# Interleaving the cross-attention output projection with the sample attention in a four-layer hybrid decoder, with one more weight slot

## The reference, cut to what matters

```python
for layer in range(DEPTH):                       # 4
    xn = rmsnorm(x, norm_mix_g[layer])
    out = rg_block(xn, ...) if layer % 2 == 0 else gla_block(xn, ...)
    x = x + out
    x = x + cross_attn(rmsnorm(x, norm_xa_g[layer]), mem_k[layer], mem_v[layer], xa_wq[layer], xa_wo[layer])
    hid = rmsnorm(x, norm_mlp_g[layer]) @ mlp_w1[layer]
    x = x + jnp.square(jax.nn.relu(hid)) @ mlp_w2[layer]

def cross_attn(xn, k, v, w_q, w_o):              # 4 heads of 256, 256 memory tokens
    q = (xn @ w_q).reshape(B, T, XA_HEADS, XA_HD)
    s = jnp.einsum('bthd,bmhd->bhtm', q, k.astype(q.dtype)).astype(jnp.float32) * (XA_HD ** -0.5)
    p = jax.nn.softmax(s, axis=-1).astype(xn.dtype)
    o = jnp.einsum('bhtm,bmhd->bthd', p, v.astype(xn.dtype)).reshape(B, T, D_MODEL)
    return o @ w_o
```

## Time and profile before

| | |
|---|---|
| time of the runs | 6314.46 and 6902.73 us, median 6608.6 |
| profiled execution | 6308.44 us; its slowest core spans 6306.9 us |
| TensorE (PE) busy | 4477.8 us, 71% |
| VectorE (DVE) busy | 3094.6 us, 49% |
| ScalarE (ACT) busy | 1959.9 us, 31% |
| GpSimd (POOL) busy | 449.1 us, 7% |
| read from and written to HBM | 452.87 MB and 35.68 MB |

### The profile page before, as it was taken

One profiled execution on the slowest core, in us unless ns is written; L12 is line 12 of the kernel. 1 busy time (PEld: TensorE's weight loads), 2 busy tenths in 40 slices (PEclk: granted clock), 3 DMA queues, 4 the chain that ended last, 5 costly groups with the idle time before them and its releaser, 6 DMA issues.

```text
span 6306.9 us, 78782 instructions; the slowest of 8 cores (6271.5 to 6306.9 us)
## 1 busy us (share of the span) xinstructions
PE 4477.8 (71%) x24832; PEld 2232.8 (35%) x24832; DVE 3094.6 (49%) x5724; ACT 1959.9 (31%) x3361; POOL 449.1 (7%) x824
## 2 busy tenths in 40 slices
PE   4443394999855569399984448499985556849996
PEld 2111143444433334344431123344433333334443
DVE  0165662545544446255565556155554444625554
ACT  2365631211322223121136654121132222412113
POOL 0111101000000000100011110100000000010000
PEclk6677695899977779599986679599987777959997
DMA  7501126222222221621210111612122222161221
GB/s 159 108 6 9 13 30 102 43 34 41 26 45 45 45 47 21 106 43 28 41 18 8 11 26 23 115 27 41 28 26 45 45 45 50 28 110 28 41 34 57
DMA packets 286689, 283.22 MB, mean 45 GB/s; under 512 B 70176, under 2 KB 219072, under 8 KB 286288
## 3 DMA queue, kind: packets, MB, share of 16 engines
q0 software_dynamic: 229616, 210.47, 22.8%
q1 hardware_dynamic: 38240, 50.92, 2.5%
q10 hardware_dynamic: 18432, 16.79, 0.9%
HBM read 452.87 MB, written 35.68 MB: 77 GB/s over the span
## 4 chain that ended last, share of the span: by engine, by line
PE 58%; DMA 17%; ACT 9%; DVE 8%; issue 7%; POOL 1%; DVEq 0%; ACTq 0%; SPq 0%; POOLq 0%
PE ps L305 56%; ACT tf L282 5%; DMA wslot<-ck 4%; DVE tf L292 3%; DMA o_Ss<-Sfs 3%; DMA wslot<-cv 2%; DMA wslot<-rg_w_in 2%; ACT L282 2%; PE ps L313 1%; ACT tb L282 1%; DVE Sb_p L292 1%; DMA o_mv<-tf 1%; DVE tf L783 1%; DMA wslot<-rg_w_a 1%; DMA wslot<-xa_wo 1%
## 5 line engine op out<-in xcount | busy, mean ns | idle before, releaser
L305 PE MATMUL ps<-xnT,wslot 128*128 128x512 bf16 (+2 forms) x9040 | 1892.1, 369 | 15.5 <-DVE tf L292 15.5
L305 PE MATMUL ps<-tb,wslot 128*128 128x512 bf16 (+2 forms) x5536 | 1079.5, 350 | 564.0 <-POOL tb L296 329.2
L282 ACT ACTIVATE tb<-ps 128x512 bf16<-128x512 f32 (+3 forms) x1074 | 572.7, 542 | 2536.4 <-PE ps L305 1763.4
L305 PEld LDWEIGHTS ps<-xnT,wslot 128*128 128x128 bf16 (+1 forms) x9040 | 854.9, 103 | 974.7 <-issue 224.7
L285 DVE TENSOR_TENSOR xT<-xT,ps 128x512 f32<-128x512 f32 (+1 forms) x1600 | 941.3, 605 | 446.7 <-PE ps L305 417.6
L305 PEld LDWEIGHTS ps<-tb,wslot 128*128 128x128 bf16 x5536 | 494.0, 98 | 1119.9 <-issue 613.2
L285 DVE TENSOR_TENSOR tb<-tb 128x512 bf16<-128x512 bf16 (+1 forms) x640 | 244.8, 385 | 736.1 <-ACT tb L282 733.2
L305 PE MATMUL ps<-actT,wslot 128*128 128x512 bf16 (+1 forms) x2560 | 486.3, 354 | 4.7 <-DMA wslot<-xa_wo 4.7
L305 PE MATMUL ps<-tb 128*128 128x8 bf16 (+4 forms) x1470 | 194.1, 230 | 263.8 <-DVE tb L288 183.8
L313 PE MATMUL ps<-identb,wslot 128*128 128x128 bf16 x1088 | 124.9, 304 | 335.8 <-DMA wslot<-cv 334.1
L282 ACT ACT_TABLE_LOAD x241 | 309.2, 1283 | 142.3 <-PE ps L305 123.8
(11 more groups left out here) (149 smaller groups left out, 3616.5 us busy)
## 6 DMA issues: line engine op xcount, KB each, us to landing
wslot<-mlp_w POOLq DMA_DIRECT2D x64, 1024.0 KB, 8.3
wslot<-ck POOLq DMA_DIRECT2D x64, 512.0 KB, 7.2
wslot<-cv POOLq DMA_DIRECT2D x64, 512.0 KB, 5.9
Sfs<-st_S ACTq DMA_DIRECT2D x128, 128.0 KB, 2.6
o_Ss<-Sfs SPq DMA_DIRECT2D x128, 128.0 KB, 2.3
tf<-xp SPq DMA_DIRECT2D x32, 256.0 KB, 11.6
wslot<-xa_wk POOLq DMA_DIRECT2D x8, 1024.0 KB, 20.7
wslot<-xa_wv POOLq DMA_DIRECT2D x8, 1024.0 KB, 14.9
```

Of the source, the lines that this page charges most:

```text
L282: P.add("act", lambda e: e.activation(out=out, in_=in_, func=func, **kw), reads, writes)
L305: ins = e.matmul(o, lhsT=l, rhs=r, start=s1, stop=s2)
```

## The change

The output projection of the four prompt tiles is no longer behind the samples. A new `oproj` does it for one half of `xa_wo`, and after every second group of 8 matmuls it calls a hook that writes one step of the sample loop: the transposes of one sample and the attention of the one before. Two steps are written ahead of the first group. The sample tile (t = 4) is projected at the end, first with the second half of `xa_wo`, which is still in its slot, then with the first half, which is loaded a second time.

In the plan the first half stands behind the second sample, the second half behind the tenth, and the first half again behind the last. A fourth slot, `wx`, lies over the buffers tf0 to tf3 (now parts of one tile) during `xa_block`; it takes pieces of samples and of `xa_wo` only. The dependencies of `wx` are those of the four tf cells. Otherwise `ahead` and the slots are as they were.

```diff
+        al = getattr(self, "alias", {})
+        if al:
+            for op in ops:
+                if any(c in al for c in op.reads):
+                    op.reads = tuple(x for c in op.reads for x in al.get(c, (c,)))
+                if any(c in al for c in op.writes):
+                    op.writes = tuple(x for c in op.writes for x in al.get(c, (c,)))
...
-        tfp = FreeList([(sb("tf%d" % i, [128, 516], F32), "tf%d" % i) for i in range(N_TF)], "tf")
+        tfbig = sb("tfbig", [128, N_TF * 516], F32)
+        tf_all = [(tfbig[:, i * 516:(i + 1) * 516], "tf%d" % i) for i in range(N_TF)]
+        tfp = FreeList(list(reversed(tf_all)), "tf")
+        slot_x = (tfbig[:, 0:2048].bitcast(BF16), "wx")
+        P.alias = {"wx": ["tf0", "tf1", "tf2", "tf3"]}
+
+        def use_slot_x(on):
+            if on:
+                for it_ in tf_all[0:4]:
+                    tfp.free.remove(it_)
+                slots.free.append(slot_x)
+            else:
+                slots.free.remove(slot_x)
+                for it_ in tf_all[0:4]:
+                    tfp.free.append(it_)
...
-                    slot = slots.get()
+                    okx = tag.startswith(("kvs", "wo"))
+                    cand = [x for x in slots.free if okx or x[1] != "wx"]
+                    if not cand:
+                        break
+                    slot = cand[0]
+                    slots.free.remove(slot)
...
                 for s in range(NSEQ_S):
                     if enabled("xa", l):
                         plan.append(("kvs%d_%d" % (l, s), kvs(s)))
-                for hf in range(2):
-                    if enabled("xa", l):
-                        plan.append(("wo%d_%d" % (l, hf), piece_cols(xa_wo[l], hf * 512, 512)))
+                        if s == 1:
+                            plan.append(("wo%d_0" % l, piece_cols(xa_wo[l], 0, 512)))
+                        if s == 9:
+                            plan.append(("wo%d_1" % l, piece_cols(xa_wo[l], 512, 512)))
+                if enabled("xa", l):
+                    plan.append(("wo%d_0b" % l, piece_cols(xa_wo[l], 0, 512)))
...
+            def oproj(slot, hf, tiles, hook):
+                wv_ = slot[0][:, 0:4096].rearrange("p (k n) -> p k n", n=512)
+                step = 0
+                for oc4 in range(4):
+                    oc = hf * 4 + oc4
+                    for t in tiles:
+                        lo, n = tcols(t)
+                        bk = banks.get()
+                        MM([(bk[0][:, 0:n], wv_[:, k, oc4 * 128:(oc4 + 1) * 128], actT[:, k, lo:lo + n],
+                             k == 0, k == NCH - 1) for k in range(NCH)], [slot[1]] + ALLA(t), [bk[1]])
+                        TT(xT[:, oc, lo:lo + n], xT[:, oc, lo:lo + n], bk[0][:, 0:n], ALU.add,
+                           [bk[1], xcell(oc, t)], [xcell(oc, t)])
+                        banks.put(bk)
+                        step += 1
+                        if hook is not None and step % 2 == 0:
+                            hook()
+
+            it = sample_iter()
+            next(it)
+            next(it)
+            so0 = ws.next("wo%d_0" % l)
+            oproj(so0, 0, range(4), lambda: next(it, None))
+            ws.release(so0)
+            so1 = ws.next("wo%d_1" % l)
+            oproj(so1, 1, range(4), lambda: next(it, None))
+            for _ in it:
+                pass
+            oproj(so1, 1, [4], None)
+            ws.release(so1)
+            so0 = ws.next("wo%d_0b" % l)
+            oproj(so0, 0, [4], None)
+            ws.release(so0)
             tbp.put(qs)
             for x_ in extra:
                 tbp.free.remove(x_)
-            out_proj(["wo%d_0" % l, "wo%d_1" % l], actT, ALLA)
...
             if enabled("xa", l):
+                use_slot_x(True)
                 xa_block(l)
+                use_slot_x(False)
```

More of the change, by code:

```diff
@@ L1198, in xa_block, with sample_iter @@
             tbp.put(kT[1])
[L1199 to L1211, removed]
+            def sample_iter():
+                pend = None
+                for s in range(NSEQ_S + 1):
+                    cur = None
+                    if s < NSEQ_S:
+                        kvslot = ws.next("kvs%d_%d" % (l, s))
+                        cur = (s, make_kT(kvslot), kvslot)
+                    if pend is not None:
+                        ps_, pk_, pslot_ = pend
+                        attention_sample(ps_, pk_, pslot_, qs, l)
+                        ws.release(pslot_)
+                        tbp.put(pk_[0])
+                        tbp.put(pk_[1])
+                    pend = cur
+                    yield
```

## The result

The changed kernel takes 6128.2 and 6130.0 us in its two undisturbed runs, where the kernel before takes 6308.8 to 6315.7: the ratio is **0.971, 95% interval 0.968 to 0.974**, so 2.9% faster (2.6 to 3.2).

The account below looks back on a forecast made before the run. The sample loop was taken as bound by ck and cv loads one after the other, with TensorE waiting. 49 - 2 - 1 - 8 = 38 us a layer, 152 in four: 6308 - 152 = 6156 us, range 6100 to 6265.

Parts of the forecast that it names:

- tail: From the last sample's transposes to the projection's end: 67.6 us falls to 18.7, saving 49 us a layer.
- overrun of pairs, 12 periods: Two projection groups ahead of each sample overrun TensorE's 5.4 us wait slightly: +2 us a layer, between -4 and +21.
- middle wo load: Second xa_wo half, behind the tenth sample's cv, makes the eleventh's ck wait for a slot: +8 us a layer.
- first wo load, fourth slot, start: First xa_wo half loads beside the third sample's ck: +1 us a layer; fourth slot and earlier first-sample loads: 0.
- third wo load: First xa_wo half, loaded again, lands before the projection's end: 0; without that cover, 10 us a layer.
- MLP start: MLP's first loads, now issued later, stay covered by 25 us of normalization: 0, otherwise a few us a layer.
- Pairs in the wait: 16 projection matmuls ahead of each sample take 5.0 to 5.7 us, just fitting TensorE's 5.4 us wait for cv.
- The step that put the clock's falls down to waits and thin work: In the sample stream, 2.5 us of waiting plus small matmuls lower TensorE's clock in many periods; the next pair restores it.
- the middle wo load costs nothing: Rival: loading xa_wo's second half during the samples is free, 8 us more saved a layer, 6124 us; chance 0.12.
- The extra slot: Fourth slot over tf0 to tf3: cross-attention keeps enough buffers, first sample's loads move about 24 us ahead: 0.
- The slower rival: Fourth slot stays out of the stream, samples have two slots: period 15.7 us, 47 lost a layer, 6496 us; chance 0.05.

## Why the prediction came out as it did

**Direction and size.** Forecast 2.4% less, 6156 us; measured 2.9% less, 6128 to 6130, inside the range. The stage gave 45 us a layer instead of 38. Term by term, for the first layer (core 2 before, core 7 after) and as the average over layers and cores:

| term | forecast | first layer | average |
|---|---|---|---|
| tail | -49 | -52.7 | -51.1 |
| overrun of pairs, 12 periods | +2 | +1 | 0 |
| middle wo load | +8 | +6.4 | +7.4 |
| first wo load, fourth slot, start | +1 | -0.9 | -0.9 |
| third wo load | 0 | 0 | 0 (0.4 by the stages) |
| MLP start | 0 | 0 | 0 |

**The tail** was priced too high, at 18.7 against 14.9 (15 to 17.7 in all layers of cores 5 and 7). The first of its pairs was given 5.4 because it "follows a wait"; it took 3.6 here, since that wait was 0.9 us. Transposes and attention took 3.0 instead of 3.7, the last attention 1.3 and the 64 small matmuls less than 4.2: all of them had been read at the low clock, or behind other work.

**Pairs in the wait** came out as predicted: 3.6 to 6.4 us, mean clock 0.83, twelve periods of 9.3. The step that put the clock's falls down to waits and thin work is borne out only in part: filling half of the wait for cv left the clock at 0.83, and with the same thin matmuls it was 0.98 without waits for loads and 1.00 with the exponential's wait filled as well. The rule of the Trainium skill that I weighed against it, "TensorE: Matmul & The Clock Gate", section "HAM oscillation — how this bites in real kernels", says every burst begins slow when a loop waits for a DMA; the trace agrees for about every second pair, and a slow beginning costs 1.5 to 2.8 us instead of 3.2.

**The middle load** had the right place and nearly the right price (6 to 7 for 8), from a mechanism that is only one of two. I had let "the slot, which is not a matter of bandwidth" stand alone; the runs show that the queue behind 1024 KB makes the same gap by itself. The 6 to 7 are the gap less a period; leaving the load out saved 10 a layer. The rival "the middle wo load costs nothing" is out.

**The extra slot** is the step that failed. "The ck and cv of the first sample move about 24 us ahead, beside nothing else: 0" priced only the first sample; the second one's load moves ahead too, and the third's ck goes out 5.2 us ahead of the first transposes instead of 1.1 behind them (core 5). By itself the slot shortens the start from 15.6 to 9.1 us and was worth 33 to 56 us in all. In the changed kernel the first pair takes most of this back. It was given no price of its own, since TensorE waited 5.0 us at that place before; but with the slot no such wait is left ahead of the third sample, and the pair costs its whole 6 us (15.0 against 9.1). Two errors of opposite sign, near -6.5 and +6 where the forecast had 0 and +1, left -0.9: that the start came out near the forecast is luck. The slot also shortens the later periods: the 13 of them take 119.0 us before, 115.3 with the slot alone, and 116.8 with the pairs and no middle load (core 5, average of the layers). So the pairs do overrun by 1 to 2 as forecast, and the slot hides it. By size, the tail, the overrun and the start are each about 2 us a layer better than forecast.

**The slower rival** was nearly exact where it was tested: 15.6 a period for 15.7, and 6520 for 6496.

## What to carry to other kernels

Interleave a compute-bound stage into a latency-bound one in bursts shorter than the measured wait, and leave the buffers of the stream alone: a buffer taken from it cost 390 us here, the interleaving gained some 140 over the slot alone. Where a burst is not covered by a wait, as the first pair here, it costs its whole time. Before that, ask what makes the wait: two loads that shared one dependency cell ran one after the other at a DMA share of 0.7, and splitting the cell gave nearly as much as the whole rearrangement. When two causes wait side by side, take both away before acquitting either.

## What the runs showed of the hardware

A load of 512 KB issued right behind one of 1024 KB on the same queue landed after 12.8 us instead of 5.7 alone, at a DMA share of 0.95 from 1048.2 to 1062.4 us (the kernel with a slot of its own for the middle load): it paid for the large one ahead of it. Each of the eight cores took in one sample's 2.1 MB in 6.3 us while the others did the same. And TensorE's clock fell again and again (0.83 on average) in a stream where it was busy for 106 of 135 us, with thin matmuls of 8 and 32 columns and waits for ScalarE and for loads between dense bursts; bursts of 16 matmuls of 512 columns took 3.6 or 4.8 to 6.5 us. At the same busy share, 73 of 92 us, but with waits of 1.4 us for ScalarE alone, it was 0.98; with that wait filled, 1.00.
